# The U and V rows of each expert laid side by side and fetched as one 8 KB row

## What is computed

```python
def _peer(xn, wq, keys, u_tab, v_tab):     # xn 512 x 1024, u_tab and v_tab (16384, 1024), float32
    q = (xt @ wq).reshape(t, PEER_HEADS, 2, PEER_HALF)
    sc = jnp.einsum('thkd,hknd->thkn', q, keys)
    s1, i1 = lax.top_k(sc[:, :, 0], PEER_TOPK)
    s2, i2 = lax.top_k(sc[:, :, 1], PEER_TOPK)
    top_s, ci = lax.top_k(cand, PEER_TOPK)          # cand: all 16 x 16 sums of s1 and s2
    experts = (i1[ci // 16] * PEER_NKEYS + i2[ci % 16])
    gates = jax.nn.softmax(top_s, axis=-1)
    ...
        act = _gelu(jnp.einsum('td,thkd->thk', xb, u_tab[eb])) * gb
        return jnp.einsum('thk,thkd->td', act, v_tab[eb])
```

## Time and profile before

| | |
|---|---|
| median of 3 runs | 3589.15 us (3585.93 to 3603.69) |
| the profiled execution | 3594.65 us, its span 3592.8 us |
| TensorE, VectorE, ScalarE, GpSimd busy | 74%, 48%, 36%, 45% of the span |
| moved by the gathers | 536.94 MB in 147456 packets |
| moved by all other DMAs | 157 MB |
| first gather issued, last sum of the experts | at 171 us, at some 1805 us |

### The profile page before, as it was taken

How to read it: one execution, slowest core, us unless ns; L and a number is a source line. 1 busy time by engine, 2 the same in 40 slices (tenths; PEclk the granted TensorE clock), 3 DMA queues, 4 the chain that set the end, 5 groups by cost and what they waited for, 6 DMA issues and landing times.

```text
span 3592.8 us, 43362 instructions
## 1 busy us (share of the span) xinstructions
PE 2642.7 (74%) x17252; PEld 2247.3 (63%) x17252; DVE 1715.0 (48%) x3881; ACT 1281.2 (36%) x1784; POOL 1618.7 (45%) x1389
## 2 busy tenths in 40 slices
PE   5521788228950686228868988888999999889999
PEld 3421577117830575116647877776999998778887
DVE  5599827884688836880026244554210113531010
ACT  2100476017720475018733322333332322533131
POOL 0045555666566655666612222222454633136463
PEclk7665899659975898659979978998999999999999
DMA  5198899999999999999912100000233322013332
GB/s 183 63 342 316 309 334 381 376 357 322 388 381 349 345 358 391 392 373 348 340 43 63 50 1 1 1 1 18 65 90 87 94 83 59 13 48 95 99 94 77
DMA packets 360653, 694.21 MB, mean 193 GB/s; under 512 B 35784, under 2 KB 215155, under 8 KB 360323
## 3 DMA queue, kind: packets, MB, share of 16 engines
q0 software_dynamic: 147456, 536.94, 40.1%
q1 hardware_dynamic: 212995, 154.50, 13.6%
HBM read 689.26 MB, written 2.10 MB: 192 GB/s over the span
## 4 chain that ended last, share of the span: by engine, by line
PE 54%; DVE 17%; issue 8%; DMA 7%; ACT 6%; another core or an unknown queue 5%; POOL 2%; SPq 0%; ACTq 0%; DVEq 0%
PE PS L1669 27%; PE PS L827 6%; DMA ring<-in_peer_v,eidx 6%; DVE ring L1389 6%; ACT ring L1025 3%; PE PS L707 2%; PE PS L878 2%; PE PS L1570 2%; POOL ring L655 1%; PE PS L1579 1%; PE PS L808 1%; PE PS L1576 1%; PE PS L1691 1%; DVE acc L2481 1%
## 5 line engine op out<-in xcount | busy, mean ns | idle before, releaser
L655 POOL DMA_INDIRECT ring<-in_peer_u,eidx x512 | 483.1, 943 | 493.9 <-DVE act_d L1389 199.7
L1669 PE MATMUL PS<-held_uH,GW 128*128 128x264 f32 (+1 forms) x3008 | 661.9, 315 | 20.1 <-POOL BIG_value L2206 16.0
L827 PE MATMUL PS<-C,ring 128*128 128x128 f32 x4096 | 543.7, 282 | 169.4 <-ACT ring L1025 90.2
L1025 ACT ACTIVATE ring<-ring,gact 128x1024 f32<-128x1024 f32 x512 | 576.3, 1147 | 222.7 <-DMA ring<-in_peer_v,eidx 168.5
L655 POOL DMA_INDIRECT ring<-in_peer_v,eidx x512 | 493.6, 964 | 328.1 <-PE PS L827 234.1
L1389 DVE CUSTOM_DVE_ANT_0 ring<-ring,PS 128x1024 f32<-128x1024 f32 x512 | 606.6, 1217 | 55.3 <-DMA ring<-in_peer_u,eidx 30.5
L2192 POOL TENSOR_TENSOR GW<-held_wr,GW 128x1024 fp32r<-128x1024 f32 x178 | 429.0, 2412 | 435.4 <-ACT GW L1961 435.4
L827 PEld LDWEIGHTS PS<-C,ring 128*128 128x128 f32 x4096 | 464.7, 144 | 245.4 <-ACT ring L1025 125.9
L1669 PEld LDWEIGHTS PS<-held_uH,GW 128*128 128x128 f32 x3008 | 503.0, 193 | 62.2 <-issue 17.1
L1669 PE MATMUL PS<-BIG_value,GW 128*128 128x264 f32 (+1 forms) x1504 | 447.2, 313 | 0.0
L1669 PE MATMUL PS<-hid,GW 128*128 128x264 f32 (+1 forms) x2304 | 366.5, 321 | 0.0
(11 more groups left out here) (465 smaller groups left out, 3480.8 us busy)
## 6 DMA issues: line engine op xcount, KB each, us to landing
held_wr<-in_w_ff SPq DMA_DIRECT2D x128, 512.0 KB, 4.0
wqr<-in_peer_wq SPq DMA_DIRECT2D x64, 512.0 KB
held_wr<-in_w_in_ab SPq DMA_DIRECT2D x18, 512.0 KB, 3.8
ring<-in_peer_u,eidx POOLq DMA_INDIRECT x512
ring<-in_peer_v,eidx POOLq DMA_INDIRECT x512
BIG<-in_w_in SPq DMA_DIRECT2D x4, 1536.0 KB, 11.6
held_wr<-in_w_qkv_c SPq DMA_DIRECT2D x12, 512.0 KB, 3.9
w_out<-in_w_out SPq DMA_DIRECT2D x1, 4096.0 KB, 19.9
```

Source lines behind the costliest of these rows:

```text
L655: e.indirect_dma_start(out=ring[:, i % RING, :], out_offset=None, in_=rows_u if k < HK else rows_v, in_offset=bass.IndirectOffsetOnAxis(ap ...
L827: ins = e.matmul(bank[6 + j // 4][:, j % 4 * P:(j % 4 + 1) * P], row[:, j * P:(j + 1) * P], ident, start=(k == 0 and j % 4 == 0), stop=(k ...
L1025: e.mul(row, row, gact[:, k:k + 1]).then_inc(*n.up(e_scaled))
L1669: ins = e.matmul(bank[b + a][:, 0:w], (hi, lo)[w_][:, k * P:(k + 1) * P], (x_hi, x_lo)[x_][:, c0:c0 + w], start=(first and w_ == 0 and x_ ...
```

## The change

The host lays the tables `peer_u` and `peer_v` side by side: expert n has one row of 2048 floats, U first. One indirect DMA gathers 128 such rows of 8 KB (1 MB) into one of five slots of 8 KB. The dot uses the first half of a slot; then gelu, gate and scaling follow on ScalarE for this pair alone, and TensorE adds the second half. The slot is free after the sum. There is one pass of 128 pairs a block instead of two of 128 rows.

The gates have to be ready by then, so they are computed in batches of heads: in block 0 for heads 0, 1, 2 to 3, 4 to 7, in the others for 0 to 3 and 4 to 7. The front of the next block and its first four heads run beside the pairs of a block, together with the block's own last four heads. `hn` is made by turning the transposed tokens on TensorE (`turn_normed`), since banks 3 and 4 are in use until the last dot of the block before. To make room, the gain `gffn` moves into the turning (a column vector in `vec`), some constants are held only during the start (`C0`), and the query weights lie in three places.

```diff
-RING = 7
+RING = 5
+AHEAD = 4
+BATCHES = [[(0, 1), (1, 2), (2, 4), (4, 8)]] + [[(0, AHEAD), (AHEAD, 8)] for blk in range(1, NB)]
...
+    def weigh():
+        while batches and heads(batches[0][0]) >= batches[0][2]:
+            batch = batches.pop(0)
+            order.extend([("shift",) + batch, ("power",) + batch])
+            weighed.append(("share",) + batch)
...
         for k in range(HK):
-            while heads(blk) < min(NH, (k + 8) // TOPK + 1):
+            need = (k + 8) // TOPK + 1
+            for h0, h1 in BATCHES[blk]:
+                if TOPK * h0 <= k + 4:
+                    need = max(need, h1)
+            while heads(blk) < min(NH, need):
                 step(others)
-                done[0] += 1
+                done += 1
+            weigh()
             order.append(("u", blk, k))
-            if k == FIRST_PART + 7:
-                while taken[("front", blk)] < FRONT_STEPS:
-                    step(others)
-                    done[0] += 1
-                order.append(("gate", blk, 0))
-            paced(others, beside_u + FRONT_STEPS - before, k, HK, done)
-        done = [0]
-        for k in range(HK):
+            if k == HK - 1 and blk < NB - 1:
+                order.append(("hn", blk + 1))
+            if k == 1 and blk:
+                order.append(("done", blk - 1))
+            shares()
             order.append(("v", blk, k))
...
+            upto = total(k + 1)
+            while done < upto:
+                step(others)
+                done += 1
...
+    early = Q_AT + 6 + Q_ROWS * AHEAD
     for blk in range(NB - 1):
         fronts.append((("front", blk + 1), FRONT_STEPS))
-        experts(blk, fronts, BESIDE_U, FRONT_STEPS - BESIDE_U)
+        rest = FRONT_STEPS - taken[("front", blk)] + early
+        experts(blk, fronts, lambda k: rest * k // HK)
...
     def first_pool(e):
         for blk in range(NB):
-            for k in range(2 * HK):
-                i = 256 * blk + k
-                if k < HK and k % TOPK == 0:
+            for k in range(HK):
+                i = HK * blk + k
+                if k % TOPK == 0:
                     e.wait_ge(r_idx, NH * blk + k // TOPK + 1)
-                slot_free(e, i)
+                if i >= RING:
+                    e.wait_ge(e_pv, i - RING + 1)
                 e.indirect_dma_start(
-                    out=ring[:, i % RING, :], out_offset=None, in_=rows_u if k < HK else rows_v,
-                    in_offset=bass.IndirectOffsetOnAxis(ap=eidx[:, blk % 2, k % HK:k % HK + 1], axis=0),
+                    out=ring[:, i % RING, :], out_offset=None, in_=pairs,
+                    in_offset=bass.IndirectOffsetOnAxis(ap=eidx[:, blk % 2, k:k + 1], axis=0),
                 ).then_inc(d_r[i % RING], 16)
...
+    def turn_normed(e, n, blk):
+
+        e.wait_ge(r_hT, 2 * blk + 2)
+        if blk:
+            e.wait_ge(e_dot, HK * blk)
+        for k in range(8):
+            ins = e.transpose(hn[:, k * P:(k + 1) * P], hnT[:, k, :], ident)
+        ins.then_inc(*n.up(e_hn))
...
-        row = ring[:, (256 * blk + HK + k) % RING, :]
-        e.wait_ge(e_scaled, HK * blk + k + 1)
+        i = HK * blk + k
+        row = ring[:, i % RING, D:2 * D]
+        if k == 0 and blk:
+            e.wait_ge(e_sum, 2 * blk - 1)
+        e.wait_ge(e_scaled, i + 1)
...
-    def scale_row(e, n, blk, k):
-        i = 256 * blk + HK + k
-        row = ring[:, i % RING, :]
-        e.wait_ge(e_gact, 2 * blk + (1 if k < FIRST_PART else 2))
-        e.wait_ge(*row_there(i))
-        e.mul(row, row, gact[:, k:k + 1]).then_inc(*n.up(e_scaled))
+    def weigh_row(e, n, blk, k):
+
+        i = HK * blk + k
+        a, row = act[:, k:k + 1], ring[:, i % RING, D:2 * D]
+        e.wait_ge(e_dot, i + 1)
+        e.activation(a, a, ACT.Gelu).then_inc(*n.up(e_gelu))
+        if k % TOPK == 0:
+            e.wait_ge(r_gate, batches_to(blk, k // TOPK))
+        e.wait_ge(e_gelu, i + 1)
+        e.mul(a, a, gate[:, blk % 2, k:k + 1]).then_inc(*n.up(e_gact))
+        e.wait_ge(e_gact, i + 1)
+        e.mul(row, row, a).then_inc(*n.up(e_scaled))
...
     def expert_dot(e, n, blk, k):
-        i = 256 * blk + k
-        row = ring[:, i % RING, :]
-        e.wait_ge(*row_there(i))
+        i = HK * blk + k
+        row = ring[:, i % RING, 0:D]
+        e.wait_ge(*pair_there(i))
...
+    arrays["in_peer_uv"] = np.concatenate([inputs["peer_u"][0], inputs["peer_v"][0]], axis=1)
```

More of the change, by code:

```diff
@@ L86, in constants @@
     two["ident"] = one["ident"]
-    two["ones"] = one["ones"]
-    return one, two
+    two["ones"] = np.ones((P, P), f)
+    return one, once, two
 def pack(parts):
@@ L176, in heads @@
         return (taken.get(("front", blk), 0) - Q_AT - 6) // Q_ROWS
-    def paced(streams, total, k, rows, done):
-        while done[0] < total * (k + 1) // rows:
-            step(streams)
-            done[0] += 1
-    def experts(blk, others, beside_u, beside_v):
-        while heads(blk) < 1:
-            step(others)
-        if blk == NB - 1:
-            order.append(("second",))
-        before = taken.get(("front", blk), 0)
-        done = [0]
-        for k in range(HK):
-            while heads(blk) < min(NH, (k + 8) // TOPK + 1):
+    batches = [(blk, h0, h1) for blk in range(NB) for h0, h1 in BATCHES[blk]]
@@ L207, in experts @@
+            if k == 1 and blk:
+                order.append(("done", blk - 1))
+            shares()
+            order.append(("v", blk, k))
+            if blk == NB - 1 and k == SECOND_AT:
+                order.append(("second",))
+                others += [(("tail", b), TAIL_STEPS) for b in range(3)] + [(("pproj", 3), 2)]
+            upto = total(k + 1)
+            while done < upto:
+                step(others)
+                done += 1
+            weigh()
         order.append(("end", blk))
@@ L684, in setup_tensor @@
             e.wait_ge(s_bt, 1 + a)
-            turn(e, bank[6 + a], ring[:, 5, 512 * a:512 * a + 512]).then_inc(*n.up(s_tp))
+            turn(e, bank[6 + a], rows[:, 5, 512 * a:512 * a + 512]).then_inc(*n.up(s_tp))
             yield
@@ L1002, in front_scalar @@
         square_mean(e, n, hs, Xb, sm[:, 5:6], sm[:, 4:5], D)
-        yield from s.to(HT + 1)
-        for half in range(2):
-            e.wait_ge(r_hTp, 2 * blk + 1 + half)
-            e.copy(W4[:, 0, 512 * half:512 * half + 512], bank[half]).then_inc(*n.up(r_hT))
-        yield from s.to(Q_AT + 2)
-        if blk:
-            e.wait_ge(e_dot, HK * blk)
-        e.copy(hn, hs).then_inc(*n.up(e_hn))
         for h in range(NH):
@@ L1300, in front_vector @@
         e.wait_ge(*now(rinv))
[L1301 removed]
+        e.tensor_scalar(hs, Xb, sm[:, 5:6], None, ALU.mult).then_inc(*up(r_hs))
+        yield from s.to(HT + 1)
+        for half in range(2):
+            e.wait_ge(*nxt(r_hTp))
+            e.tensor_tensor(hnT[:, 4 * half:4 * half + 4, :], f4(bank[half]), vp(76 + 4 * half, 4), ALU.mult).then_inc(*up(r_hT))
         s16 = tk[:, 0:32].rearrange("p (a k) -> p a k", a=2)
@@ L1443, in first_vector @@
                 expert_dot(e, n, *name[1:])
-            elif name[0] == "gate":
-                weigh_vector(e, n, *name[1:])
-            elif name[0] == "end":
+            elif name[0] == "shift":
+                shift_vector(e, n, *name[1:])
+            elif name[0] == "share":
+                share_vector(e, n, *name[1:])
+            elif name[0] == "done":
                 experts_done(e, n, name[1])
```

239 lines of the change are left out of this document (123 added, 116 removed).

## The result

The changed kernel took 3625.6 us (median of four runs, 3622.4 to 3637.7) beside 3587.5 us for the kernel before on the same chip (four runs, 3581.4 to 3603.7): the ratio is 1.0105, 95% interval 1.0065 to 1.0146. It is slower by 1%, where 2.5% faster was forecast, and outside the range. The kernel before differs from chip to chip (3530 to 3535 us on some, 3587 on others); the changed kernel took 3626, 3631 and 3626 us on the three chips where it ran, so where the kernel before takes 3530 the ratio is 1.028 (e5, e18). I did not look for the cause of that.

The account below looks back on a forecast made before the run. It took DMA row transfers as the bound, VectorE beside heads and S5: blocks of 401, 750 (two) and 378 make 1529 us for 1636, 106 saved, less 17 for the clock: 3505.6 profiled, median 3500, range 3405 to 3600.

Parts of the forecast that it names:

- A pair takes 2.56 us by DMA: Gathers: a pair of 1.049 MB takes 2.56 us at 409 GB/s, the fastest rate that gathers have had.
- Dot 1.30, GpSimd free enough, 106 table loads: Pair loop: VectorE's dot costs 1.30 us, GpSimd's 512 issues cost nothing, ScalarE's table loads rise from 59 to 106.
- The wait for scores, 2.2 us a head, 59 us: Heads: VectorE stands still 2.2 us a head for TensorE's scores, 59 us for 27 heads.
- 155 us for 48: Blocks 1 and 2, beside eight heads: 48 pairs take 155 us of VectorE, against 144 us for rows and query weights.
- The other 49 pairs go by DMA: 125. With 10 us for what a block boundary and the single waits cost: Blocks 1 and 2, away from heads and S5: 49 pairs take 125 us, boundary and waits 10, the block 375.
- it hides, but lengthens the way through a slot: ScalarE's work, some 250 of 375 us a block, hides but lengthens the way through a slot.
- The second rival: Slot ring: five slots held through five steps, 16.5 us a turn, 3.3 us a pair, slower at 3645 us; chance 0.17.
- Its sign: Slices away from heads stay under 370 GB/s with all compute engines below 80%.
- The least turn: Slot ring: one slot's shortest way round takes some 10 us, 2.0 us a pair, so no bound.
- The clock: 17 us: TensorE at heads: a low clock makes the wait 0.64 us longer at each of 27 heads, 17 us.
- The third rival: TensorE's clock stays at 1.2 GHz and TensorE becomes the bound, 387 us a block; median 3520 us; chance 0.10.
- The fourth rival: DMA: busy time is per byte, so at most 79 us can be gained and about 10 come back: 3580; chance 0.08.

Follow-up runs that it names:

- e5: The changed kernel run again with nothing edited, on a second chip: 3630.6 us, ratio 1.0276 to the kernel before.
- e18: The changed kernel run again with nothing edited, on a third chip: 3626.4 us, ratio 1.0278 to the kernel before.
- e3: The changed kernel with all front steps of a block put ahead of its pairs, so pairs run alone: 4077 us (one run).
- e7: The changed kernel with VectorE's top-k of a head two steps later: 3591.9 us, 39 less.
- e1: The changed kernel without the input projection's products for six of the eight k: 3585.2 us, 43 less.
- e6: The changed kernel with 12 empty steps in a front, between steps that wait for one another: 3598.3 us, 32 less.
- e13: The changed kernel with six slots (one table for sine and cosine), 12 empty front steps and top-k two steps later: 3501.6 us, 126 less.
- e4: The changed kernel without each pair's gelu and gate factor: 3535.0 us, 93 less.
- e12: The changed kernel with squares in place of the square roots in the norms of fronts and tails: 3592.0 us, 36 less.
- e9: The changed kernel with six slots instead of five, one table serving sine and cosine: 3566.9 us, 61 less.
- e10: The changed kernel with four slots instead of five: 3780.7 us (one run), 153 more.

## Why the prediction was wrong

**A pair takes 2.56 us by DMA: right.** Alone 2.57 us at 403 to 407 GB/s (e3). Halving the packets won nothing more: the earlier trace rows had 409.

**Dot 1.30, GpSimd free enough, 106 table loads: right** (1.214 + 0.082, 0.96 an issue, 106 loads in the whole trace).

**The wait for scores, 2.2 us a head, 59 us: right.** 57.0 us in 22 waits, and it was on the path: removing it gave 39 us (e7). That the sums agree so well is in part luck: 27 waits of 2.2 us were forecast, 22 of 2.6 came. Beside heads 3.1 us a pair where 155 us for 48, 3.2, was forecast.

**"The other 49 pairs go by DMA: 125. With 10 us for what a block boundary and the single waits cost": this step failed.** It costed TensorE at nothing and the front's waits at next to nothing. The projections had stood in the U pass, where TensorE had little else (40 of 160 us busy), no sum waited behind them and no slot hung on ScalarE. Now each stands between a sum and the slot it frees. In the three stretches a pair cost some 4.1 us where the forecast took 2.56 for most of them. Blocks 0, 1 and 2 took 438, 416 and 412 us where 401, 375 and 375 were forecast, block 3 384 to its last gather and 397 to its last sum, where 378 was. Of the loss the projection's width is 43 us (e1) and the distance of one step between the engines 32 (e6); no run has both, and together they don't make the 121 us between the forecast's 3505.6 and the profiled 3626.3. The two kinds of stops and a sixth slot do: e13, with one table less, is 126 us faster than the changed kernel.

**ScalarE: "it hides, but lengthens the way through a slot": only the second half was right, and I gave it no price.** Gelu and gate with the table loads that they bring cost 93 us (e4), the roots' table loads alone 36 (e12), on an engine that is 59% busy.

**The second rival came true**, with chance 0.17: slower, with a turn of 16.2 us where it said 16.5 and 3.23 us a pair where it said 3.3; 3626 us where it said 3645. Its sign, slices away from heads under 370 GB/s with every engine below 80%, is what 690 to 800 shows. That its turn came so near is luck, since its parts were off. It missed two things. The least turn isn't 10 us but 12.9 (e3): I took the first gather of all, 5.7 us to its dot, with the DMA idle; in the stream it is 6.7 to the last packet and 1.2 more to the dot. With that, the forecast's own numbers leave nothing: 12.9/5 is 2.6 us, and each microsecond that an engine's queue adds to the turn costs 0.2 a pair. The queues added 3.3 us, not 6.5. Had I put the turn at 12.9 and added only the waits for scores (57 us) and the half front step that a row finds before it on VectorE, this would have been the likeliest case. And the slots aren't all of it: a sixth lengthens the turn (18.8) and gives 61 us, and VectorE's waits for the front stay as long (e9).

**The clock: 17 us, neither shown nor excluded.** It was 0.78 in the mean over the pairs. The third rival (1.2 GHz throughout) didn't happen. Low clock makes a sum 1.76 us (e3), 1.4 in the changed kernel, 0.90 at full clock: 0.5 us of the turn, some 0.1 us a pair and some 50 us in all if all of it counts. No run separated it.

**The fourth rival** (busy DMA time is mostly work) was partly right about the mechanism that gives it no gain: the change took only 42 us of transfer time away, 1399 us for 1441 (40.1% of 3592.8), and new gaps took more than that.

Two slips in the prediction change nothing here: the range counts 216 pairs that go by DMA where the sum has 237, and rival 2's own numbers give 3643 us, not 3645.

Open: why an even spread of steps beats one by weight and two steps of lag beat four, and why the kernel before differs by 1.6% between chips when the changed one doesn't.

## What to carry over

When passes are merged and every buffer goes through all engines, work out a buffer's turn first, with latencies as they are in the loaded stream (measure the loop alone, as e3 does), and divide by the number of buffers: if that is already the pace of the bound, a stop of any engine in the ring has no slack to hide in, and part of it is paid, however idle that engine is. Then look at which other work each engine's queue puts between two steps of the ring, and keep steps that wait for one another two or three rounds apart; that alone gave 2% here without removing any work. More buffers and fewer stops were nearly separate gains here, and memory that is free for only part of the time is enough for the first.

## What the runs showed of the hardware that I had not expected

A gather of 1 MB in 8 KB rows takes 6.7 us from issue to its last packet when two or three are under way, although they come every 2.57 us (e3), 6.6 us with four slots (e10), and 7.3 to 8.1 us in the others of the table. Table loads cost 1.283 us, and the next instruction starts 0.01 us behind one. The kernel with 4 KB rows took 3530 to 3587 us from chip to chip (six groups of runs), the one with 8 KB rows 3626 to 3631 (three); nothing here shows that the rows are the reason.
